# Layer norms computed in two halves of the tokens in a four-layer transformer kernel

## The reference, cut to what matters

```python
def rms_norm(x, gain):                       # layers 0 and 1, before mixer and feed-forward, and at their end
    return x * lax.rsqrt(jnp.mean(x * x, axis=-1, keepdims=True) + 1e-6) * gain

def layer_norm(x, g, b):                     # layers 2 and 3, after mixer and after feed-forward
    mu = x.mean(-1, keepdims=True)
    var = jnp.square(x - mu).mean(-1, keepdims=True)
    return (x - mu) * lax.rsqrt(var + 1e-5) * g + b

# layers 0 and 1:  x = x + mixer(rms_norm(x));  x = x + conv_ffn(rms_norm(x));  then rms_norm(x, final)
# layers 2 and 3:  h = layer_norm(ALPHA * h + mixer(h));  h = layer_norm(ALPHA * h + conv_ffn(h))
```

## Time and profile before

| | us |
|---|---|
| median of 3 runs | 2559.25 (2557.65 to 2562.07) |
| the profiled execution | 2565.07 |
| its span, first to last instruction | 2563.2 |
| TensorE busy | 2477.6 (97%) |
| GpSimd busy | 1804.1 (70%) |
| VectorE busy | 1336.2 (52%) |
| ScalarE busy | 802.9 (31%) |

### The profile page before, as it was taken

How to read it: one execution, slowest core, us unless ns; L and a number is a source line. 1 busy time by engine, 2 the same in 40 slices (tenths; PEclk the granted TensorE clock), 3 DMA queues, 4 the chain that set the end, 5 groups by cost and what they waited for, 6 DMA issues and landing times.

```text
span 2563.2 us, 33687 instructions
## 1 busy us (share of the span) xinstructions
PE 2477.6 (97%) x11702; PEld 2062.1 (80%) x11702; DVE 1336.2 (52%) x2041; ACT 802.9 (31%) x1718; POOL 1804.1 (70%) x1589
## 2 busy tenths in 40 slices
PE   9989899999999899999999989999999999999997
PEld 7878788888877788888878877888877887788886
DVE  7777755666027556663177765333116455534312
ACT  3367733111017731110045643111005563311101
POOL 7866777666667876666688987666677658766664
PEclk9999999999999999999999999999999999999999
DMA  4300013223321033323222212323322222223332
GB/s 144 115 25 26 26 42 99 94 94 98 99 75 66 26 107 98 98 94 99 91 82 66 66 51 81 98 92 97 99 90 68 67 75 66 79 94 98 98 98 75
DMA packets 58115, 208.59 MB, mean 81 GB/s; under 512 B 6496, under 2 KB 6752, under 8 KB 58016
## 3 DMA queue, kind: packets, MB, share of 16 engines
q1 hardware_dynamic: 57744, 206.88, 25.0%
q10 hardware_dynamic: 272, 0.39, 0.1%
HBM read 205.09 MB, written 2.16 MB: 81 GB/s over the span
## 4 chain that ended last, share of the span: by engine, by line
PE 77%; DVE 9%; POOL 6%; ACT 6%; issue 1%; DMA 1%; ACTq 0%; DVEq 0%; SPq 0%; POOLq 0%
PE PS L854 24%; PE PS L856 24%; PE PS L855 24%; POOL WL L589 2%; ACT GP L1691 2%; POOL WH L587 1%; DVE GTL L2391 1%; DVE PC L2583 1%; PE PS L1254 1%; DVE NM L2335 1%; ACT MP L1913 1%; DMA raw<-stream 1%; POOL RQ L652 1%; POOL RQ L645 0%; PE PS L1049 0%
## 5 line engine op out<-in xcount | busy, mean ns | idle before, releaser
L589 POOL TENSOR_TENSOR WL<-raw,WH 128x1024 fp32r<-128x1024 f32 x380 | 922.4, 2427 | 31.7
L854 PE MATMUL PS<-HH,WH 128*128 128x512 f32 x2272 | 900.2, 396 | 26.9 <-DVE HL L2166 12.4
L856 PE MATMUL PS<-HH,WL 128*128 128x512 f32 x2272 | 890.9, 392 | 0.0
L855 PE MATMUL PS<-HL,WH 128*128 128x512 f32 x2272 | 890.4, 392 | 0.0
L854 PEld LDWEIGHTS PS<-HH,WH 128*128 128x128 f32 x2272 | 429.7, 189 | 125.8 <-issue 23.2
L856 PEld LDWEIGHTS PS<-HH,WL 128*128 128x128 f32 x2272 | 429.8, 189 | 91.3
L855 PEld LDWEIGHTS PS<-HL,WH 128*128 128x128 f32 x2272 | 430.3, 189 | 86.6 <-issue 1.0
L586 POOL TENSOR_TENSOR WH<-raw,SC 128x32 fp32r<-128x32 f32 x380 | 112.5, 296 | 499.1 <-DMA raw<-stream 483.9
L587 POOL TENSOR_SCALAR WH<-raw 128x992 fp32r<-128x992 f32 x380 | 406.9, 1071 | 0.0
L854 PE MATMUL PS<-GH,WH 128*128 (+1 forms) x704 | 275.5, 391 | 0.0
L855 PE MATMUL PS<-GL,WH 128*128 (+1 forms) x704 | 273.9, 389 | 0.0
(11 more groups left out here) (355 smaller groups left out, 3363.4 us busy)
## 6 DMA issues: line engine op xcount, KB each, us to landing
raw<-stream SPq DMA_DIRECT2D x380, 512.0 KB, 3.5
X<-x SPq DMA_DIRECT2D x4, 512.0 KB, 5.0
out<-X SPq DMA_DIRECT2D x8, 256.0 KB, 2.1
PR<-params SPq DMA_DIRECT2D x1, 536.0 KB, 8.3
spare_raw_nsa<-stream SPq DMA_DIRECT2D x1, 512.0 KB, 3.7
spare_raw_swa<-stream SPq DMA_DIRECT2D x1, 512.0 KB, 4.7
spare_raw_diff<-stream SPq DMA_DIRECT2D x1, 512.0 KB, 4.4
spare_raw_fox<-stream SPq DMA_DIRECT2D x1, 512.0 KB, 4.6
```

The lines of the kernel that those rows point to most:

```text
L589: pool.tensor_tensor(WL[:, w], raw[:, w], hi.bitcast(F32), ALU.subtract).then_inc(chunk_split, 1)
L854: pe.matmul(to, h, his[k], start=start and k == 0, stop=False)
L855: pe.matmul(to, h, los[k], start=False, stop=False)
L856: last = pe.matmul(to, l, his[k], start=False, stop=stop and k == n_k - 1)
```

## The change

Six of the nine norms (`HALVED` = 2, 4, 5, 6, 7, 8) are computed separately for tokens 0 to 255 (left, z = 0) and 256 to 511 (right, z = 1).

- **The products ahead of the norm.** Where a feed-forward ends (norms 2, 4, 6, 8), the last one or two down chunks (`HALVED_CHUNKS` = 1, 1, 2, 2) are multiplied first for the left half of all four output tiles and then for the right (`down_halved`), as matmuls of 256 columns. Ahead of norms 5 and 7 the last chunk of the out projection is halved, the right half into PSUM bank 3.
- **The sums.** `norm_sums` of the left half stands inside the right half's products, that of the right half inside the first products after the norm. `keep_busy` is no longer called in norms.
- **The products after the norm.** `first_two_halved`: all 8 tiles of the left half, then all 8 of the right, for two chunks, in matmuls of 256 columns.
- **Shares.** In the RMS norms 2 and 4 GpSimd writes the left low parts of tiles 1, 3, 5, 7; the right half is normalised into PSUM and all its low parts are VectorE's. In the layer norms GpSimd centres tiles 6 and 7 only, and takes the normalised tile and the low part of tiles 3, 5, 7 (norm 6, right: tile 3 alone).
- **Splits.** Ahead of a mixer GpSimd splits two chunks before its share of the norm and the third after it; before, all three came first.
- **diff's opening.** `lambdas()` on VectorE and its exponential on ScalarE come after the first rotary embedding instead of before it; TensorE's wait for `padded` moves to just before the first scores.
- **Output.** 16 DMAs of 128 KB in place of 8 of 256 KB.

```diff
+HALVED = (2, 4, 5, 6, 7, 8)
+TAIL = {0: 8, 2: 4, 4: 4, 5: 7, 6: 4, 7: 7, 8: 4}
+POOL_TILES = {0: ((1, 3, 5, 7), ()), 1: ((), ()), 2: ((1, 3, 5, 7), ()), 3: ((), ()), 4: ((1, 3, 5, 7), ()),
+              5: ((3, 5, 7), (3, 5, 7)), 6: ((3, 5, 7), (3,)), 7: ((3, 5, 7), (3, 5, 7)), 8: ((3, 5, 7), (3, 5, 7))}
+NORMED_BANK = (1, 2, 3, 5)
+HALVED_CHUNKS = {2: 1, 4: 1, 6: 2, 8: 2}
-CENTRED_BY_DVE = 4
+CENTRED_BY_DVE = 6
...
 # GpSimd, ahead of a mixer
-                    split(done, q["proj_chunk"] + 3)
-                    norm_lo(2 * n)
+                    split(done, q["proj_chunk"] + 2)
+                    norm_rest(2 * n)
+                    split(q["proj_chunk"] + 2, q["proj_chunk"] + 3)
...
 # TensorE
+            def first_two_halved(c, k_norm, banks, sums_ahead):
+                pe.wait_ge(chunk_split, c + 2)
+                for k in range(CT):
+                    if k == sums_ahead:
+                        norm_sums(k_norm, 1)
+                    halves_of(c, k_norm, banks, k, 0)
+                for k in range(CT):
+                    halves_of(c, k_norm, banks, k, 1)
...
-                if 0 < k < 8:
-                    keep_busy(0, 18 if ln else 12)
...
+                        for z in range(2):
+                            bank = RIGHT_OUT_BANK if z else out_bank(q["kind"], t)
+                            for k in range(KT):
+                                if k == 6 - 6 * z:
+                                    first_sums(k_norm, z)
+                                if z == 1 and k == 3:
+                                    norm_sums(k_norm, 0)
+                                last = products((c + t) % SLOTS, bank_part(bank, z), [part_of(HH, k, z)], [part_of(HL, k, z)], 1,
+                                                k == 0, k == KT - 1, k)
...
 # ScalarE, the last norms' order (tail = 7: norms 5 and 7; tail = 4: the others)
+                if tail == 4:
+                    square(k, 4, 1)
+                    if ln:
+                        means(k, 0)
+                        square(k, 5, 1)
+                    row_factor(k, 0)
+                    if not ln:
+                        square(k, 5, 1)
+                    norm_tiles(k, 0, 0, 2)
+                    square(k, 6, 1)
+                    square(k, 7, 1)
+                    norm_tiles(k, 0, 2, 4 if ln else 6)
+                    if ln:
+                        means(k, 1)
+                        norm_tiles(k, 0, 4, 6)
+                else:
+                    means(k, 0)
+                    row_factor(k, 0)
+                    square(k, 7, 1)
+                    norm_tiles(k, 0, 0, 4)
+                    means(k, 1)
+                    norm_tiles(k, 0, 4, 6)
+                row_factor(k, 1)
+                norm_tiles(k, 0, 6, KT)
+                norm_tiles(k, 1, 0, KT)
...
 # VectorE, diff's opening
                 pad()
-                lambdas()
                 rope_k(0)
                 rope_q(0)
                 rest_q(0)
+                lambdas()
...
 # VectorE, after the last out tile (k = 5 and 7)
+                variance(k, 0)
+                centre(k, 0, 0)
+                centre(k, 1, 0)
+                dve.wait_ge(chunk_used, c + OUT_TILES - 1)
+                residual(n, q, RIGHT_OUT_BANK, OUT_TILES - 1, 1)
+                norm_tiles(k, 0, 0, 6)
+                variance(k, 1)
+                centre(k, 0, 1)
+                centre(k, 1, 1)
+                norm_tiles(k, 0, 6)
+                norm_tiles(k, 1)
```

More of the change, by code:

```diff
@@ L1497, in feed_forward @@
                             down(kk, i, False, False)
-                    down_last(per_half - 2)
+                    if half == 0:
+                        down_last(per_half - 2)
+                    else:
+                        halved = HALVED_CHUNKS[2 * n + 2]
+                        for kk in range(per_half - 2, per_half - halved):
+                            down(kk, 0, False, False)
+                        down_halved(range(per_half - halved, per_half))
                     c += per_half
@@ L1577, in norm @@
[L1577 to L1582 removed]
+                    square(k, t, None)
+                for h in range(LATE_AHEAD, KT):
+                    late_hi(k, h)
@@ new lines, in down, with first_norm @@
+                norm_tiles(k, 0, 0, 2)
+                accumulate(k, 5, 1)
+                add(7, 1)
+                accumulate(k, 6, 1)
+                norm_tiles(k, 0, 2, 6)
+                if ln:
+                    variance(k, 1)
+                    centre(k, 0, 1)
+                    centre(k, 1, 1)
+                norm_tiles(k, 0, 6)
+                norm_tiles(k, 1)
+            def first_norm():
+                for t in range(KT):
+                    accumulate(0, t)
+                dve.wait_ge(inputs_landed, 16 * 2)
+                norm_tiles(0, None)
@@ L2785, in _ @@
                 if n == 0:
[L2786 to L2790 removed]
+                    first_norm()
                     dve.wait_ge(tables_landed, 16 * 3)
@@ L2809, in _ @@
                 down(n, q)
-            norm(8)
 def rotary_order():
```

580 lines of the change are left out of this document (373 added, 207 removed).

## The result

The changed kernel takes 2566.3 us, median of 16 runs (2563.8 to 2569.0), against 2559.2 for the kernel before, also 16 runs (2557.2 to 2564.8). The ratio is 1.0024, interval 1.0017 to 1.0031: about 6 us slower by the ratio, 7.1 by the two medians. The forecast was 8 us faster, and the time lies above its range.

A forecast was written before the change was run, and what follows sets the result against it. TensorE, carrying 77% of the chain of waits, was taken as the bound. Terms 2.7 + 2.5 + 0.6 + 0.5 + 0.3 + 1.4 = 8.0 us off the 2559.25 median gave 2551, range 2539 to 2563.

The forecast's parts named there:

- the third chunk at 20.8: Norms 2 and 4: TensorE's third chunk begins 20.8 us behind the last down chunk's start, against 24.4, 3.6 earlier.
- the 2.7 that were forecast: Norm 2 with swa's opening: 3.6 us won in the norm, 0.9 lost as the rotary starts later, 2.7 left.
- the walk: Step-by-step timing of each halved norm over the engines' queues, mostly to TensorE's third chunk, with low parts at 0.42 us.
- covered: GpSimd's third split ends before it is needed: 33.9 against 34.6 in norm 6, 18 against 20.8 in norms 2 and 4.
- `lambdas`, moved behind it, no longer stands in the way: Diff's opening: first rotary step ready 3.4 us earlier, VectorE free some 2 earlier, lambdas behind it; 2.5 taken as won.
- The 2.5 us: Norm 4 with diff's opening: 2.5 us taken as won.
- Rival 4: Openings of swa and diff, tied to GpSimd, eat the norms' gain: only 2.8 us won, 2556.5; chance 13%.
- rival 2: Without keep_busy TensorE stays at 1.2 GHz in norms 5 to 7: 2.4 us slower, 2561.7; chance 12%.
- granted clock 1.00 in norms 5 to 7: Sign expected in the profile after: TensorE at full clock in the three layer norms between blocks.
- The prices: Half-wide operations: X or HH 0.50 us apart instead of 0.71, products 0.12 apart, GpSimd's centring 0.65.
- the term of 0.5 us won: Norm 6: end at 34.6 against 35.5, taken as 0.5 us won, bounds -3 and 7.
- rival 1: VectorE and GpSimd block each other in layer norms, 5 us each for norms 5, 6, 7: 8.4 slower, 2567.7; chance 15%.

The follow-up runs named there:

- early memsets: Four of the six memsets opening fox moved into the down products of diff's feed-forward, on top of norm 6 mended: 0.9986 of the kernel before, against 1.0010 without.
- three splits first: GpSimd splits three chunks before its share of norms 2 and 4, against the kernel with norms 5 to 7 whole and lambdas later: 0.9991 of before, against 0.9974.
- norm 6 mended: Changed kernel with lambdas after diff's first factor, right tiles 3, 5, 7 of norm 6 on GpSimd, and fox's third split first: 1.0010 of the kernel before.
- lambdas back: Changed kernel with diff's lambdas and their exponential ahead of the first rotary embedding again: 1.0031 of the kernel before.

## Why the prediction was wrong

**Norms 2 and 4.** Forecast: the third chunk at 20.8 behind the start of the last down chunk. Measured 21.6 and 21.8 against 24.4 before. TensorE's opening of swa lost 0.1 (from the third chunk to the first scores 13.37 before, 13.51 after) where I had 0.9, so norm 2 gave the 2.7 that were forecast. That the term came out is luck: the norm won 0.8 less than the walk said and the opening lost 0.8 less. The gain hangs on the split's new place, which I had only as "covered": with the old order norm 2's stretch is as long as it was whole and the stage of norm 4 shows -1.0 in place of -3.3.

**Diff.** "`lambdas`, moved behind it, no longer stands in the way" was wrong. I looked at VectorE, where it leaves a gap free, and not at ScalarE's queue, in which the moved exponential stands ahead of evacuations. The 2.5 us reach the third chunk and are given back at 1302. Rival 4 said that openings would eat the gain; it was right for diff in what it cost, though it named GpSimd as the cause and the wait was for `lambdas`, and it was wrong for swa.

**Norms 5 and 7.** The walk held until its last third. Norm 5, changed kernel:

```profile
1537.17 0.60 ACT L1757 ACTIVATE X<-WK,PR 128x256 f32<-128x256 f32 x1
...
1549.26 0.60 ACT L1757 ACTIVATE X<-WK,PR 128x256 f32<-128x256 f32 x1 [0.43 <-DVE WK L2438]
```

```profile
1554.97 0.74 POOL L729 TENSOR_TENSOR HL<-X,HH 128x256 fp32r<-128x256 f32 x1 [0.71 <-ACT HH L1760]
```

```profile
1557.34 0.40 PE L973 MATMUL PS<-HH,WH 128*128 128x512 f32 x1
```

With 0 at 1527.04, the first left X starts at 10.1 (forecast 10.1), the waits of ScalarE for VectorE are 0.4 as forecast, ScalarE ends at 27.8 (26.8), the last low part at 28.7 (27.5), the third chunk is at 30.3 (28.2). One us is ScalarE's: for the second factor it waits 0.87 for the variance. The last 1.6 are TensorE's (forecast 0.7), with the clock at half from 1548 to 1554.8; in norm 7, at full clock, they are 0.9. In nine other executions with the same norm 5 the stretch took 29.55 to 29.59 in six, 30.0 in two, which had no drop there, and 30.4 in one, which had the same long drop. So a drop of 6.8 us costs 0.7 to 0.8: rival 2 in direction, a fifth of its size, and not tied to `keep_busy`, since before had its own drop there with it. The forecast's sign "granted clock 1.00 in norms 5 to 7" held in norm 7 alone (0.89, 0.91, 1.00). The prices held: X and HH start 0.50 apart and products 0.12; GpSimd's half-wide centring took 0.73 where I had taken 0.65.

**Norm 6.** This is the step that failed: the term of 0.5 us won, which came out as 11.6 us lost. The forecast had the first low part at 14.7, the end of the right sums at 19.8, the end at 34.6, and a third split that ends at 33.9, "covered". Measured 15.5, 22.2 and 43.1; the third and fourth split ran from 33.4 to 41.0. Four faults:

- *The cover was looked for on the wrong engine.* No product waited for the third split. But the earlier trace rows was before my eyes, and I set it against every low part (rival 1, with short GpSimd operations) and not against the two splits that the change lays beside the last low parts. Rival 1 was right in mechanism and wrong in place: 0.7 us in norms 5 and 7 for which it had 5 each, 5.6 in norm 6, where it had 5 too but from short operations and not from the splits.
- *The share.* With one right tile on GpSimd, VectorE has seven of eight low parts there. The walk priced them at 0.42 each. From the right factor to VectorE's end it took 15.4 us, and 10.4 with two of them given away. How much of the 5.0 is the share and how much that the splits then start behind the last low part stays open.
- *The walk ended at TensorE's third chunk.* For norms 2 and 4 I followed VectorE into the next layer; for norm 6 I didn't, although fox opens with 7 us of memsets on VectorE, the longest of all. The early memsets show what that is worth: 4 us with the norm and the splits the same.
- *The clock.* The walk had TensorE at full clock. In six of the eight profiles with norm 6 halved the right sums ran wholly or in part at half, which cost 0.9 to 1.3 us between the first sum and ScalarE; the changed kernel's was one of them.

In the sum: the terms were -2.7, -2.5, -0.6, -0.5, -0.3 and -1.4, together -8.0; by the table's stages they came to -3.0, +0.2, +1.2, +11.6, +0.5 and -0.9, together +9.6. Of the 17.6 between them norm 6 is 12.1, diff 2.7 and norms 5 and 7 are 2.6. (The spans differ by 10.1; the two executions stand 1.8 below and 1.2 above their medians, which leaves the 7.1 between the medians.) Two of the rows hold the clock of that one execution: norm 5 reads +0.3 to +0.5 in eight of nine other profiles, and norm 6 +11.6, +12.4 and +13.8 in the three kernels that leave it as the change has it.

The Trainium skill ("SBUF — State Buffer", section "Who interferes with whom") states that a VectorE instruction with two SBUF inputs and a GpSimd instruction that reads SBUF hold each other, and that issue order decides who waits. The low parts and the adds behave so here: 2.25 and 2.30 us against 0.41. The same section says that an instruction with at most one SBUF input doesn't contend, outside the modes in which VectorE uses both of its ports. The trace of the kernel with three splits first agrees: VectorE's residual at 749.31, with one operand in PSUM, takes its 0.42 inside the subtraction that began at 748.72, and the add behind it, with both in SBUF, is held. The condition on the modes matters: in the kernel with norm 6 mended a TENSOR_SCALAR of 16x512 with one SBUF input was held (2.46 us from 1934.37, 0.41 alone).

**Norm 8.** 27.7 against 27.5 forecast. All eleven kernels of the experiments that change something halve norm 8 in the same way. In seven of their profiles its stage is 1.2 to 1.4 shorter than before; in the four others TensorE's clock dropped 12 to 14 us ahead of the end, the right sums ran on half the clock, and the gain is nothing (-0.2 to +0.2).

**The base.** The sum was made against an execution that turned out 7.6 us over another one. Terms read as differences inside norms were hurt little, since these stages agree to 0.6 us.

## What to carry to other kernels

Ask of each moved long operation not only who waits for its result, but whose operations it now lies beside: a 2.4 us GpSimd split turned 0.41 us low parts into 2.3 us, and with the third split in its old place norms 2 and 4 took 24.4 and 24.3 us again, 1.3 of it by one held add and the rest in a stretch of half clock. Follow a shortened or lengthened stage to the engine that opens the next one; a walk that ends where TensorE starts again misses that. When two traces are compared, look first at the clock where the wait ends: 1.3 us of a loss that looked like the order of the splits was the clock. And when something is moved on one engine, read the queue of the engine that answers it: both have to be free at the new place.

## What the runs showed that I had not expected

- A memset of 2 partitions by 1024 takes as long as one of 64 by 1024: 0.91 us, and 1.16 from start to start.
- VectorE operations on a single column are held as long as wide ones by a GpSimd operation: 1.73 and 1.76 us for a subtraction of one number per partition, which took 0.16 where nothing ran beside it (lambdas back) and 0.50 in the kernel before, beside the shorter first part of a split.
- Two executions of one kernel differed by 7.6 us in span, half of it between two posts that hold a stretch of 147 us where the granted clock was 0.95 in one and 0.98 in the other.
